# Expert blocks in order of token count, three of them with high and low halves side by side as one stationary operand

## The chip, the core and the metric

The kernel runs on one NeuronCore of a Trainium2 chip. The time is the device time of one execution in microseconds (us), median of several runs.

## What is computed

A decoder trunk of two layers for 256 tokens of 1024 channels: a mixer (convolution, pooling, mLSTM), cross-attention into 256 memory tokens, and a channel mixer that is a dense SwiGLU in the first layer and a mixture of experts in the second. The change touches the experts alone. Cut to them:

```python
logits = xt @ router_w                      # xt: 256 tokens x 1024
top_v, top_e = lax.top_k(logits, 2)         # two of eight experts a token
gate = jax.nn.softmax(top_v, axis=-1)
# rows are packed into blocks of 128 that each belong to one expert
def expert_block(args):
    xblk, e = args
    return (jax.nn.silu(xblk @ w1[e]) * (xblk @ w3[e])) @ w2[e]
y = segment_sum(yb * slot_w[:, None], slot_tok, num_segments=256)
```

w1 and w3 are 1024 x 3584 for each expert, w2 is 3584 x 1024, all float32. With the inputs that the reference makes, the reference's router gives the eight experts 76, 57, 68, 47, 42, 82, 54 and 86 rows.

## The kernel before, in words

**Precision.** A product of float32 matrices is made of three fp32r matmuls: each operand is split into a high half (a copy rounded to fp32r, by ScalarE) and a low half (the difference, by VectorE), and high x high, high x low (activation low with weight high) and low x high (activation high with weight low) are added up in PSUM. The helper `three` does this, lines 1898 to 1900.

**The expert stage** begins about 1010 us into the span and takes the rest. There are eight blocks, one for each expert in the order of their numbers; each holds up to 128 rows (`SLOTS`). Should an expert have more, further blocks follow after the eighth; there are none with these inputs.

A block is 42 chunks of weights (`ESEQ`, `N_EXP`), each 128 x 2048 floats, 1 MB. They come in seven groups: two chunks of w1, two of w3, and, from the second group on, two of w2 that belong to the group before; the last w2 chunks come at the end. A chunk goes through four hands, each an engine with its own queue in program order:
- SP issues the load (`expert_load`, line 596) into one of six buffers (`e_raw`: three named raw, then mem_t, area and xf), as soon as the buffer's last chunk has been split by VectorE.
- ScalarE makes the high half (`e_split`, line 771) into one of three `w_hi` buffers, as soon as TensorE is done with the chunk three back.
- VectorE makes the low half (`lo`, line 1214) into one of three `w_lo`.
- TensorE multiplies (`e_chunk`): 4 k-tiles or column parts by three matmuls of 512 columns, 12 a chunk. The activations (`x_hi`, `x_lo`, or `hid_e`) are the stationary operand, 128 x 128, the weights the moving one.

In ScalarE's and VectorE's queues the splits are mixed with what must be done with results (`e_post`). In step t they split chunk t and do the post work of chunk t-3; as a rule the split stands first. Post work of a group: SiLU of the w1 result out of PSUM (line 1134), the product with the w3 result (line 1747), then a **turn**: TensorE transposes the 128 x 512 product (`turn`, line 2317, four transposes, issued behind the second w1 chunk of the next group), ScalarE takes the high half (line 1139) and VectorE the low half, which the w2 chunks need.

At the end of a block ScalarE scales half of the output rows by the gates (line 1121), VectorE the other half (line 1735), and POOL adds the 128 rows to a sum in DRAM by an indirect DMA (line 714). The next block's rows are selected ahead of time (`select`, `slot_rows`), fetched by another indirect DMA on POOL (line 710), turned by TensorE (`turn_rows`, line 2399) and split (`gather_hi`, line 1115; `gather_lo`). Before the last block VectorE makes the tables for further blocks (`further_blocks`, lines 1823 to 1839). Blocks 0 to 6 are a loop on each engine; the last, with the final norm behind it, is written out.

## Time and profile before

| | |
|---|---|
| Time, median of 3 runs | 1989.75 us (1989.38 to 1990.35) |
| Span of the profiled execution | 1986.5 us |
| Instructions in it | 31923 |
| TensorE busy | 1969.3 us, 99% |
| VectorE busy | 1638.9 us, 82% |
| ScalarE busy | 1288.2 us, 65% |
| DMA, mean over the span | 268 GB/s |
| Granted TensorE clock, mean | 0.999 |
| Splits of weights by VectorE, mean | 2260 to 2292 ns |

The time of a run includes the launch and the end around the program; the profiled execution has no time of its own in the results, so its span of 1986.5 us stands beside the runs' median of 1989.75 us. In the page PE is TensorE's matmuls, PEld its weight loads, DVE VectorE, ACT ScalarE, POOL GpSimd, SP the engine that issues loads. Matmuls overlap in the records, so a matmul's record is longer than the distance to the next one's start. Tiles bear the names under which they were allotted: a_hi and a_lo hold the activations' halves, z_sig the hidden product, h the rows, k_t and u_pad small tables.

### The profile page before, as it was taken

Reading aid. Unit: us, or ns where it says so; the run is one execution under the profiler, and the core shown is the slowest. Engines: PE = TensorE matmul, PEld = TensorE weight load, DVE = VectorE, ACT = ScalarE, POOL = GpSimd, SP = SyncE. Lnnn points to the kernel's source line nnn. Section 1 sums busy time; section 2 is a strip of 40 time slices with the busy share of each in tenths; the row PEclk is TensorE's granted clock in tenths of the full one; section 3 lists DMA queues with packets and bytes.
Section 4 is the critical chain, followed back from the end, with each engine's and each line's share of the span. In section 5 each row is a group of like instructions: output and inputs, shape, how many; then the busy total and the mean of one; then the engine's idle time right before and its main releaser. Section 6 shows DMA issues by size and latency. Waiting matters only on the chain.

```text
span 1986.5 us, 31923 instructions
## 1 busy us (share of the span) xinstructions
PE 1969.3 (99%) x12185; PEld 1767.6 (89%) x12185; DVE 1638.9 (82%) x1702; ACT 1288.2 (65%) x1155; POOL 46.3 (2%) x89
## 2 busy tenths in 40 slices
PE   9999999999999999999999999999999999999998
PEld 8999999989999999999988888888888888888886
DVE  6999967577778988976578888988989888888986
ACT  7666555444436666564467777878778787777775
POOL 0000000000000000000000000000000000000000
PEclk9999999999999999999999999999999999999999
DMA  8545556445555545555479999999999999999994
GB/s 269 171 133 184 166 173 199 143 160 194 192 176 170 170 133 170 191 182 186 136 290 382 374 381 384 361 385 358 388 379 369 381 362 385 372 380 385 359 392 170
DMA packets 311377, 533.26 MB, mean 268 GB/s; under 512 B 14363, under 2 KB 157363, under 8 KB 311271
## 3 DMA queue, kind: packets, MB, share of 16 engines
q1 hardware_dynamic: 308550, 523.71, 74.8%
q0 software_dynamic: 2720, 8.08, 1.5%
q8 instruction: 73, 1.20, 0.3%
q14 instruction: 34, 0.27, 0.0%
HBM read 526.30 MB, written 7.34 MB: 269 GB/s over the span
## 4 chain that ended last, share of the span: by engine, by line
PE 88%; DVE 6%; ACT 2%; issue 2%; SPq 1%; DMA 0%; DVEq 0%; ACTq 0%
PE ps L1898 26%; PE ps L1900 26%; PE ps L1899 26%; PE ps L2213 4%; DVE w_lo L1214 2%; PE ps L2215 2%; ACT w_hi L764 1%; PE ps L2317 1%; DVE c L1281 1%; PE ps L2067 1%; PE ps L2087 1%; DVE xf L1299 0%; PE ps L2399 0%; PE ps L2033 0%; SPq L511 0%
## 5 line engine op out<-in xcount | busy, mean ns | idle before, releaser
L1214 DVE TENSOR_TENSOR w_lo<-raw,w_hi 128x2048 fp32r<-128x2048 f32 (+1 forms) x330 | 745.2, 2260 | 190.4 <-ACT w_hi L764 131.1
L1898 PE MATMUL ps<-w_hi,a_hi 128*128 128x512 f32 (+1 forms) x1472 | 568.0, 386 | 1.1 <-DVE w_lo L1214 1.1
L1900 PE MATMUL ps<-w_hi,a_lo 128*128 128x512 f32 (+1 forms) x1472 | 560.8, 381 | 0.0
L1899 PE MATMUL ps<-w_lo,a_hi 128*128 128x512 f32 (+1 forms) x1472 | 559.8, 380 | 0.0
L1898 PE MATMUL ps<-a_hi,w_hi 128*128 128x256 f32 x1456 | 416.2, 286 | 2.0 <-DVE a_lo L1569 1.6
L1899 PE MATMUL ps<-a_lo,w_hi 128*128 128x256 f32 x1456 | 411.9, 283 | 0.0
L1900 PE MATMUL ps<-a_hi,w_lo 128*128 128x256 f32 x1456 | 411.8, 283 | 0.0
L771 ACT ACTIVATE w_hi<-raw 128x2048 fp32r<-128x2048 f32 x168 | 322.3, 1919 | 119.8 <-PE ps L1900 119.2
L764 ACT ACTIVATE w_hi<-raw 128x2048 fp32r<-128x2048 f32 x157 | 296.3, 1894 | 56.7 <-PE ps L1900 52.1
L1898 PEld LDWEIGHTS ps<-w_hi,a_hi 128*128 128x128 f32 x1472 | 276.7, 188 | 54.5 <-DVE w_lo L1214 3.7
L1900 PEld LDWEIGHTS ps<-w_hi,a_lo 128*128 128x128 f32 x1472 | 276.5, 188 | 53.8
L1899 PEld LDWEIGHTS ps<-w_lo,a_hi 128*128 128x128 f32 x1472 | 276.9, 188 | 50.7 <-issue 0.2
L1898 PEld LDWEIGHTS ps<-a_hi,w_hi 128*128 128x128 f32 x1456 | 278.9, 192 | 3.7 <-issue 2.0
L1899 PEld LDWEIGHTS ps<-a_lo,w_hi 128*128 128x128 f32 x1456 | 279.0, 192 | 0.4
L1900 PEld LDWEIGHTS ps<-a_hi,w_lo 128*128 128x128 f32 x1456 | 278.9, 192 | 0.0
L1214 DVE TENSOR_TENSOR w_lo<-mem_t,w_hi 128x2048 fp32r<-128x2048 f32 x56 | 128.3, 2292 | 16.3 <-ACT w_hi L771 16.3
L1214 DVE TENSOR_TENSOR w_lo<-area,w_hi 128x2048 fp32r<-128x2048 f32 x56 | 128.3, 2291 | 15.6 <-ACT w_hi L771 15.0
L1214 DVE TENSOR_TENSOR w_lo<-xf,w_hi 128x2048 fp32r<-128x2048 f32 x56 | 128.0, 2286 | 15.8 <-ACT w_hi L771 15.8
L771 ACT ACTIVATE w_hi<-area 128x2048 fp32r<-128x2048 f32 x56 | 107.6, 1921 | 42.5 <-PE ps L1900 42.5
L1898 PE MATMUL ps<-b_pair,w_hi 128*128 128x256 f32 x456 | 130.3, 286 | 0.4 <-DVE b_pair L1214 0.4
L1899 PE MATMUL ps<-b_pair,w_hi 128*128 128x256 f32 x456 | 129.0, 283 | 0.0
L1900 PE MATMUL ps<-b_pair,w_lo 128*128 128x256 f32 x456 | 129.0, 283 | 0.0
(357 smaller groups left out, 2313.3 us busy)
## 6 DMA issues: line engine op xcount, KB each, us to landing
raw<-in_moe_w SPq DMA_DIRECT2D x168, 1024.0 KB, 7.0
raw<-in_w_in SPq DMA_DIRECT2D x66, 1024.0 KB, 5.2
mem_t<-in_moe_w SPq DMA_DIRECT2D x56, 1024.0 KB, 6.8
area<-in_moe_w SPq DMA_DIRECT2D x56, 1024.0 KB, 6.9
xf<-in_moe_w SPq DMA_DIRECT2D x56, 1024.0 KB, 6.7
raw<-in_ffn_w SPq DMA_DIRECT2D x33, 1024.0 KB, 5.3
raw<-in_w_mlstm_out SPq DMA_DIRECT2D x8, 1024.0 KB, 5.1
raw<-in_w_out SPq DMA_DIRECT2D x8, 1024.0 KB, 5.9
```

Of the source, the lines that this page charges most:

```text
L764: act.activation(w_hi[c % SPL][:, 0:n], raw[c % RAW][:, 0:n], ACT.Copy).then_inc(hi_done.sem, 1)
L771: act.activation(w_hi[m % SPL][:, :], e_raw[m % ERAW][:, 0:CH], ACT.Copy).then_inc(e_hi.sem, 1)
L1214: return dve.tensor_tensor(dst, whole, as_f32(hi), ALU.subtract)
L1281: ins = dve.scalar_tensor_tensor(dst, src, tap, dst, ALU.mult, ALU.add)
L1898: pe.matmul(dst, wh, xh, start=start, stop=False, skip_group_check=True)
L1899: pe.matmul(dst, wh, xl, start=False, stop=False, skip_group_check=True)
L1900: return pe.matmul(dst, wl, xh, start=False, stop=stop, skip_group_check=True)
L2067: ins = pe.matmul(ps[4 + hd % 2][:, tt * T:(tt + 1) * T], q_t[:, k, tt * P:(tt + 1) * P], k_t[:, k, :], start=(tt == 0 and e == 0), stop=( ...
L2087: ins = pe.matmul(ps[X_OUT_BANK[hd]][:, e * T:(e + 1) * T], vx[:, m, hd, e * P:(e + 1) * P], z_sig[:, 4 + 2 * (hd % 2) + m, :], start=(e = ...
L2213: pe.matmul(b[:, :].rearrange("p (a t) -> p a t", a=2), wh[:, k, cols], b_pair[:, :, k, :], start=(k == 0), stop=False, skip_group_check=True)
L2215: ins = pe.matmul(b[:, 0:T], wl[:, k, cols], b_hi[:, k, :], start=False, stop=(k == KB - 1), skip_group_check=True)
L2317: ins = pe.transpose(ps[6][:, k * P:(k + 1) * P], act_e[g % 2][:, k * P:(k + 1) * P], ident[:, :])
```

## The change

- **Order and kinds of blocks.** Block 0 stays expert 0. For the other seven, a plan on VectorE ranks experts by their count and puts the three smallest in blocks 1, 3 and 5 (`KINDS`, `PLACES`, L for light, H for heavy). SP reads the expert's number of a block from a table (`expert_of`) and so begins block 1's loads only when the plan is done. Light blocks hold 64 rows, heavy ones 128; an expert with more would get a further block (`cap` in `further_blocks`).
- **Light blocks on TensorE.** The stationary operand is 64 columns of high half beside 64 of low half (`x_both`, `hid_both`). It is multiplied by the weights' high half and by their low half: 8 matmuls of 512 columns a chunk instead of 12. The result has the high half's product in rows 0 to 63 and the low half's in rows 64 to 127.
- **Joining the two.** ScalarE copies each w1 and w3 result to SBUF (`up_copy`, `gate_copy`, 128 x 512). `turn_fold` multiplies it by a 128 x 64 matrix `fold` (two identities above each other), which turns and adds the halves: eight real fp32 matmuls of 64 columns where four transposes stood. SiLU and product then work on 128 x 256. At the block's end ScalarE copies rows 64 to 127 of the output, VectorE adds rows 0 to 63 (`y_low`), and ScalarE scales both halves of 64 rows.
- **Order in the light block's queues.** On both engines the post work of chunk t-3 stands ahead of the split of chunk t, always.
- **The loop** is over three pairs of a heavy and a light block; blocks 6 and 7, both heavy, are written out. The output addition of a light block has 64 rows.
- **Rows for the next block** are split into `x_both`, `x_hi`/`x_lo`, or what the next block's kind needs (`kinds`).
- Small: constants on POOL for the plan; one semaphore fewer for the constants, three fewer for loads.

The diff, cut to its core:

```diff
+LIGHT = 64
+KINDS = "HLHLHLHH"
+N_LIGHT = KINDS.count("L")
+N_PAIRS = 3
+N_OVER = 4
...
+def block_places():
+    light, heavy = iter(range(1, 1 + N_LIGHT)), iter(range(1 + N_LIGHT, NE))
+    return [0] + [next(light if kind == "L" else heavy) for kind in KINDS[1:]]
...
 # SP
+            sp.wait_ge(ids_done, 1)
+            with sp.Fori(1, NE - 1) as b:
+                e = expert_of(b)
+                for m in range(N_EXP):
+                    expert_load(b, m, e)
...
 # ScalarE
+            def l_post(b, j, m, kinds):
+                kind, g, i = ESEQ[m]
+                if m == N_EXP - 1:
+                    for n, done in enumerate((y_half.at(b, 1), None)):
...
+                        act.activation(y_low[:, n * 512:(n + 1) * 512], ps[4 + n][LIGHT:P, :], ACT.Copy).then_inc(l_copied.sem, 1)
+                    for n in range(2):
+                        c = slice(n * 512, (n + 1) * 512)
+                        act.wait_ge(l_y_sum.sem, l_y_sum.at(j, n + 1))
+                        act.activation(y_rows[0:LIGHT, c], y_low[:, c], ACT.Copy, scale=gate_col[0:LIGHT, :]).then_inc(ye_done.sem, 1)
+                    return
+                act.wait_ge(e_pe.sem, e_pe.at(b, m + 1))
+                if kind != "w2" and i == 1:
...
+                    act.activation(dst[g % 2], ps[(2 * g + (kind == "w3")) % 4][:, :], ACT.Copy).then_inc(l_copied.sem, 1)
...
+                if m in turned:
+                    n = turned[m]
+                    act.wait_ge(e_turned.sem, e_turned.at(b, n + 1))
+                    act.activation(act_l[n % 2], ps[6][:, 0:T], ACT.Silu).then_inc(e_silu.sem, 1)
+                    act.wait_ge(e_gated.sem, e_gated.at(b, n + 1))
+                    act.activation(hid_both[n % 2][:, :, 0, :], act_l[n % 2].rearrange("p (k s) -> p k s", k=4), ACT.Copy).then_inc(e_hid_hi.sem, 1)
...
+            def l_block(b, j, kinds):
+                for t in range(SPL, N_EXP + SPL):
+                    l_post(b, j, t - SPL, kinds)
+                    if t < N_EXP:
+                        e_split(b, t)
+                    else:
+                        e_split(b + 1, t - N_EXP)
...
 # VectorE
+                if m == N_EXP - 1:
+                    for n in range(2):
+                        c = slice(n * 512, (n + 1) * 512)
+                        dve.wait_ge(l_copied.sem, l_copied.at(j, 2 * NGE + n + 1))
+                        dve.tensor_tensor(y_low[:, c], y_low[:, c], ps[4 + n][0:LIGHT, :], ALU.add).then_inc(l_y_sum.sem, 1)
+                    return
...
+                    dve.wait_ge(e_silu.sem, e_silu.at(b, n + 1))
+                    dve.tensor_tensor(act_l[n % 2], act_l[n % 2], ps[6][:, T:2 * T], ALU.mult).then_inc(e_gated.sem, 1)
+                    dve.wait_ge(e_hid_hi.sem, e_hid_hi.at(b, n + 1))
+                    lo(hid_both[n % 2][:, :, 1, :], act_l[n % 2].rearrange("p (k s) -> p k s", k=4), hid_both[n % 2][:, :, 0, :]).then_inc(e_hid_lo.sem, 1)
...
+            def plan():
+                ch.link(dve.tensor_copy(total, ps[5][:, 32:32 + NE]))
+                ch.link(dve.scalar_tensor_tensor(key, total, float(NE), iota8, ALU.mult, ALU.add))
...
+                ch.link(dve.tensor_tensor(picked, each, which, ALU.mult))
+                ch.link(dve.tensor_reduce(by_block[:, :, 1:NE], picked[:, :, 1:NE, :], AX, ALU.add))
+                dve.tensor_copy(ids[0:1, 1:NE], ids_f[0:1, 1:NE]).then_inc(ids_done, 1)
...
+                ch.link(dve.tensor_scalar(cap, place, N_LIGHT + 0.5, -float(SLOTS - LIGHT), ALU.is_lt, ALU.mult))
...
 # TensorE
+            def turn_fold(b, j, g):
+                pe.wait_ge(l_copied.sem, l_copied.at(j, 2 * g + 2))
+                if g:
+                    pe.wait_ge(e_gated.sem, e_gated.at(b, g))
+                for n, src in enumerate((up_copy, gate_copy)):
+                    for k in range(4):
+                        c = n * T + k * LIGHT
+                        ins = pe.matmul(ps[6][:, c:c + LIGHT], src[g % 2][:, k * P:(k + 1) * P], fold[:, :],
+                                        start=(n == 0 and k == 0), stop=True, skip_group_check=True)
+                ins.then_inc(e_turned.sem, 1)
...
+                    for k in range(4):
...
+                        pe.matmul(dst, both, wh[:, c], start=(i == 0 and k == 0), stop=False, skip_group_check=True)
+                        ins = pe.matmul(dst, both, wl[:, c], start=False, stop=(i == 1 and k == 3), skip_group_check=True)
...
-            with pe.Fori(0, NE - 1) as b:
-                e_block(b)
+            with pe.Fori(0, N_PAIRS) as i:
+                e_block(2 * i)
+                l_block(2 * i + 1, i)
+            e_block(NE - 2)
             e_block(NE - 1, True)
```

How the instructions now stand, at the two places of which the prediction speaks. REGISTER_ALU rows compute a semaphore's value.

ScalarE around a turn, before: a_hi at L1139 is the high half of the turned product, z_sig at L1134 the SiLU.

```order
L771 ACTIVATE w_hi<-raw 128x2048
L1134 ACTIVATE z_sig<-ps 128x512
L1139 ACTIVATE a_hi<-ps 128x512
L768 REGISTER_ALU
L771 ACTIVATE w_hi<-mem_t 128x2048
```

and in a light block of the change (L1225 the copy of the w1 result to SBUF, L1230 the SiLU, L1232 the high half):

```order
L807 ACTIVATE w_hi<-raw 128x2048
L1220 REGISTER_ALU
L1225 ACTIVATE cacc<-ps 128x512
L1229 REGISTER_ALU
L1230 ACTIVATE z_sig<-ps 128x256
L1232 ACTIVATE a_hi<-z_sig 128x4x64
L807 ACTIVATE w_hi<-raw 128x2048
```

The SiLU moved behind the turn, next to the high half, and VectorE's product stands between the two:

```order
L1298 TENSOR_TENSOR w_lo<-raw,w_hi 128x2048
L1876 REGISTER_ALU
L1880 REGISTER_ALU
L1881 TENSOR_TENSOR z_sig<-z_sig,ps 128x256
L1298 TENSOR_TENSOR a_hi<-z_sig,a_hi 128x4x64
L1298 TENSOR_TENSOR w_lo<-raw,w_hi 128x2048
```

This is VectorE of a light block; L1881 is the product, the row behind it the low half. ScalarE's high half waits for L1881, the row behind L1881 for ScalarE's high half, and both stand ahead of the next split of their engine.

ScalarE where a light block ends (vx is `y_low`, h the rows of the output, L1155 the next block's rows):

```order
L1155 ACTIVATE a_hi<-ps 128x512
L803 ISA
L804 ISA
L807 ACTIVATE w_hi<-raw 128x2048
L1220 REGISTER_ALU
L804 REGISTER_ALU
L807 ACTIVATE w_hi<-raw 128x2048
L1214 ACTIVATE vx<-ps 64x512
L1211 REGISTER_ALU
L1214 ACTIVATE vx<-ps 64x512
L1218 ACTIVATE h<-vx,k_t 64x512 x2
L804 REGISTER_ALU
```

Before, one activation of 128 x 512 (L1121) stood there; now there are four of 64 x 512, two of which wait for VectorE, ahead of the split of the next block's chunk 2. VectorE has its two sums at the same place:

```order
L1298 TENSOR_TENSOR w_lo<-raw,w_hi 128x2048
L1873 ISA
L1874 TENSOR_TENSOR vx<-vx,ps 64x512
L1873 REGISTER_ALU
L1874 TENSOR_TENSOR vx<-vx,ps 64x512
L1308 REGISTER_ALU
L1298 TENSOR_TENSOR w_lo<-raw,w_hi 128x2048
```

They stand behind its split of chunk 1 and ahead of that of chunk 2, where one scaling of 128 x 512 stood before.

## Rows read from the trace of the kernel before

**Rows 1.** The page, parts 1 and 2: TensorE's busy time, its granted clock in 40 slices.
```profile
PE 1969.3 (99%) x12185; PEld 1767.6 (89%) x12185; DVE 1638.9 (82%) x1702; ACT 1288.2 (65%) x1155; POOL 46.3 (2%) x89
...
PEclk9999999999999999999999999999999999999999
```
**Rows 2.** Waits inside one expert block, 1133.1 to 1252.4 us: total, times, longest.
```profile
ACT w_hi L771 <- PE ps L1900: 25.7, 36, 1.3
DVE w_lo L1214 <- ACT w_hi L771: 12.0, 26, 1.4
```
**Rows 3.** Windows in that block: engines' busy time, TensorE's granted clock, DMA share, GB/s.
```profile
1133.10:1252.41 119.31, 119.31 (x546) 98.48 (x545) 106.78 (x68) 91.52 (x62) 4.88 (x2) 1.00 1.02 377
1140.00:1151.50 11.50, 11.50 (x51) 9.29 (x50) 9.41 (x5) 10.46 (x7) 2.13 (x1) 1.00 1.03 339
1151.50:1164.90 13.40, 13.40 (x62) 11.05 (x61) 12.57 (x14) 9.76 (x9) 0.00 (x0) 1.00 1.05 395
1193.00:1200.00 7.00, 7.00 (x33) 5.79 (x32) 6.64 (x4) 5.40 (x3) 2.09 (x1) 1.00 0.99 359
```
**Rows 4.** Timeline of TensorE around a turn: start us, us, engine, line.
```profile
1245.41 0.39 PE L1900 MATMUL ps<-w_hi,a_lo 128*128 128x512 f32 x1
1245.64 0.60 PE L2317 MATMUL ps<-ident,z_sig 128*128 128x128 f32 x4
1246.00 0.48 PE L1898 MATMUL ps<-w_hi,a_hi 128*128 128x512 f32 x1
```
**Rows 5.** Timeline of VectorE where one block's chunks give way to the next's.
```profile
1244.56 0.68 DVE L1747 TENSOR_TENSOR z_sig<-z_sig,ps 128x512 f32<-128x512 f32 x1
1245.16 2.29 DVE L1214 TENSOR_TENSOR w_lo<-area,w_hi 128x2048 fp32r<-128x2048 f32 x1
...
1252.41 4.66 DVE L1214 TENSOR_TENSOR w_lo<-raw,w_hi 128x2048 fp32r<-128x2048 f32 x2
1256.99 0.74 DVE L1735 TENSOR_SCALAR h<-ps,k_t 128x512 f32<-128x512 f32 x1
1257.65 2.28 DVE L1214 TENSOR_TENSOR w_lo<-raw,w_hi 128x2048 fp32r<-128x2048 f32 x1
```
**Rows 6.** Timeline of ScalarE over the same stretch.
```profile
1246.34 0.60 ACT L1139 ACTIVATE a_hi<-ps 128x512 fp32r<-128x512 f32 x1 [1.21 <-PE ps L2317]
1246.83 1.91 ACT L771 ACTIVATE w_hi<-xf 128x2048 fp32r<-128x2048 f32 x1
...
1250.46 1.92 ACT L771 ACTIVATE w_hi<-raw 128x2048 fp32r<-128x2048 f32 x1
1252.83 1.92 ACT L771 ACTIVATE w_hi<-raw 128x2048 fp32r<-128x2048 f32 x1 [0.45 <-PE ps L1900]
...
1257.35 1.28 ACT L771 ACT_TABLE_LOAD   x1
```
**Rows 7.** Timeline of TensorE: the first gather, 16 fp32 matmuls in 32 passes.
```profile
1011.85 3.81 PE L2305 MATMUL ps<-vx,q_t 128*128 128x128 f32 x32 [0.55 <-ACT q_t L1170]
```
**Rows 8.** Groups by line of VectorE in that block: busy us, mean ns, idle before.
```profile
L1700 DVE TENSOR_SCALAR vx<-k_t,u_pad 128x128 f32<-128x128 f32 x2 | 0.6, 340 | 0.0
```
**Rows 9.** Timeline at the start of the first block, VectorE and TensorE.
```profile
1021.04 0.16 DVE L1850 COPY u_pad<-ps 128x8 f32<-128x8 f32 x1
1021.43 2.29 DVE L1214 TENSOR_TENSOR w_lo<-mem_t,w_hi 128x2048 fp32r<-128x2048 f32 x1 [0.23 <-ACT w_hi L771]
...
1016.42 0.50 PE L1898 MATMUL ps<-w_hi,a_hi 128*128 128x512 f32 x1
```
**Rows 10.** Timeline of VectorE ahead of the last block; waits from 1853 to 1866 us.
```profile
1856.38 0.17 DVE L1823 TENSOR_SCALAR u_pad<-u_pad 128x8 f32<-128x8 f32 x1
1856.59 0.17 DVE L1824 TENSOR_TENSOR_SCAN u_pad<-u_pad 128x8 f32<-128x8 f32 x1
...
PEld ps L1898 <- DVE w_lo L1214: 1.5, 1, 1.5
```
**Rows 11.** DMA issues from 1145.5 to 1147 us: one load, KB, us from issue to landing.
```profile
area<-in_moe_w SPq DMA_DIRECT2D x1, 1024.0 KB, 8.2
```

More of the change, by code:

```diff
@@ L314, in trunk @@
         warm = table(1)
+        key, place, cap, place_of = (table(NE) for _ in range(4))
+        plan_room = dec[:, :, :].rearrange("p a b -> p (a b)")
+        beats, chosen = (plan_room[:, f * NE * NE:(f + 1) * NE * NE].rearrange("p (a b) -> p a b", a=NE) for f in range(2))
+        picked = plan_room[:, 2 * NE * NE:(2 + 1 + 3 * TT) * NE * NE].rearrange("p (r a b) -> p r a b", r=1 + 3 * TT, a=NE)
+        fold = sb("fold", [P, LIGHT])
         ids = sb("ids", [1, 16], I32)
@@ L1156, in e_block @@
                     if first:
-                        e_post(b, t - SPL, last)
+                        e_post(b, t - SPL, last, kinds)
                     if t < N_EXP:
@@ L1752, in e_post, with e_block, next_rows @@
                     lo(hid_e[n % 2][1].rearrange("p k s -> p (k s)"), ps[6][:, :], hid_e[n % 2][0].rearrange("p k s -> p (k s)")).then_inc(e_hid_lo.sem, 1)
-                if (kind, g, i) == ("w3", 1, 1) and not last:
+                if not last:
+                    next_rows(b, m, kinds)
+            def e_block(b, last=False, kinds="L"):
+                for t in range(SPL, N_EXP + SPL):
+                    first = ESEQ[t - SPL] in POST_FIRST
+                    if first:
+                        e_post(b, t - SPL, last, kinds)
+                    if t < N_EXP:
+                        e_split(b, t)
+                    if not first:
+                        e_post(b, t - SPL, last, kinds)
+                    if t >= N_EXP and not last:
+                        e_split(b + 1, t - N_EXP)
+            def next_rows(b, m, kinds):
+                if ESEQ[m] == ("w3", 1, 1):
                     slot_gates(b)
@@ L1765, in e_block, with l_block @@
+            def l_block(b, j, kinds):
                 for t in range(SPL, N_EXP + SPL):
-                    first = ESEQ[t - SPL] in POST_FIRST
-                    if first:
-                        e_post(b, t - SPL, last)
+                    l_post(b, j, t - SPL, kinds)
                     if t < N_EXP:
                         e_split(b, t)
-                    if not first:
-                        e_post(b, t - SPL, last)
-                    if t >= N_EXP and not last:
+                    else:
@@ L1849, in _ @@
             slot_rows(0, ps[5][:, 64:67])
-            ch.link(dve.tensor_copy(total, ps[5][:, 32:32 + NE]))
+            plan()
             def tail(b):
@@ new lines, in l_block @@
+            def l_block(b, j):
+                for m, (kind, g, i) in enumerate(ESEQ):
+                    l_chunk(b, j, m)
+                    if m == ROWS_AT:
+                        slot_rows(b + 1, ps[7][:, 0:3])
+                    if kind == "w1" and i == 1 and g:
+                        turn_fold(b, j, g - 1)
+                    if (kind, g, i) == TURN_LAST:
+                        turn_fold(b, j, NGE - 1)
+                    if (kind, g, i) == ("w2", NGE - 2, 1):
+                        turn_rows(b)
```

197 lines of the change are left out of this document (139 added, 58 removed).

## Prediction

> **What bounds the kernel now.** I read the page first for the engines and the clock. TensorE is busy for 99% of the span, and its granted clock is in the top tenth in every slice [rows 1]. That alone doesn't say that it is the bound, so I took one block of the expert stage, from the start of its first weight split on VectorE to that of the next block, and asked who waits for whom. ScalarE waited 25.7 us for TensorE in it, VectorE 12.0 us for ScalarE, and TensorE next to nothing [rows 2]. TensorE has work for all 119.31 us [rows 3]. Matmuls of 512 columns start 0.23 us apart and four transposes take 0.36 us [rows 4]: 36 transposes and the slot rows come to some 4 us, and the other 115.3 us are 504 matmuls at 0.228 each. So a block is as long as TensorE needs, 119.3 us.
>
> The others are close behind, and the prediction rests on that. The DMA engines moved 377 GB/s in the block at a share of 1.02 [rows 3], which is 44.98 MB. Where nothing but weights moved and the queue was full, it was 395 GB/s at 1.05; beside the two indirect transfers 339 GB/s for 11.5 us and 359 GB/s for 7.0 us. A block that waited for DMA alone would take 18.5 us for those two stretches (6.41 MB) and 38.57 MB / 395 = 97.6 us for the rest: 116.1 us. VectorE was busy for 106.8 us of the block [rows 3].
>
> A rule speaks against the change here. The Trainium skill, "DMA: Bandwidth & Descriptors", Specifications, gives about 358 GB/s as the HBM limit of a core. By that a block could not be shorter than 44.98 MB / 358 = 125.7 us, which is above what is measured; the trace disagrees, and the measurement decides. With the page's figure a light block could gain nothing.
>
> **The light block, part by part.** A chunk goes from 12 matmuls to 8: 1.82 us instead of 2.74, 38 us of TensorE less in a block. TensorE stops being the bound, so the gain is not 38 us; the next chain sets it. I work out VectorE's, per group of six chunks, counting from the start of VectorE's split of chunk A (the second w1 chunk, behind which the turn stands). Splits follow each other at 2.20 us (a record lasts 2.29; operations of 512 columns follow at 0.60) [rows 5]. ScalarE's split takes 1.92, another operation can follow it or a copy 0.1 us before its end, and VectorE's split starts 1.95 after ScalarE's [rows 6].
> - VectorE splits A, B, C at 0, 2.20 and 4.40 and is free at 6.60.
> - TensorE has A multiplied at 2.29 + 0.06 + 7 x 0.228 + 0.39 = 4.3. Then the fold: eight real fp32 matmuls, which go in two passes each. 32 such passes took 3.81 us [rows 7], so 16 take 1.8: done at 6.1. ScalarE's SiLU of 256 columns (0.37 by the slope between 512 and 2048 columns) is done at 6.5.
> - VectorE's product 6.60 to 7.0, ScalarE's high half 7.05 to 7.45, and only behind it ScalarE's split of D, at 7.37. VectorE's split of D starts at 9.32, not 6.60.
> - E, F and the next A: 11.5, 13.7 and 15.9.
>
> A turn so costs VectorE 2.7 us, most of it waiting, because product, high half and the next split stand in one line over two in-order engines; before, turns lay under TensorE's time. A group takes 15.9 us against 17.0, seven groups 111.
>
> At the start, the heavy block's last matmul slot ends at T0 = 1255.2; VectorE's splits of chunks 1 and 2 then start at T0 - 0.4 and T0 + 2.45 [rows 5]. The split of chunk 41 starts at 2.45 + 39 x 2.20 + 7 x 2.7 + 1.55 = T0 + 108.8. The 1.55 is row selection and slot rows: two operations of 0.34 [rows 8] and six of 0.1 to 0.2. They were free under TensorE and now count.
>
> **The handover to the heavy block** loses part of it. Behind split 41 VectorE first takes two x parts (1.2 us); chunk 0 reaches TensorE 5.75 us after the start of split 41, at T0 + 114.55, 1.6 us after TensorE ran dry. Then the output: where one ScalarE and one VectorE operation stood there are now two ScalarE copies, two VectorE sums behind split 1, and two scalings, all ahead of ScalarE's split of chunk 2. They have 64 rows by 512 columns; I price them as the 512-column operations of 128 rows, the nearest rows (0.5 on ScalarE, 0.6 on VectorE). Counted from split 41: sums at 7.8 and 8.4, scalings at 8.5 and 9.1, split 9.65, VectorE's split 11.6 to 13.9. TensorE has used up chunks 0 and 1 at 11.2: 2.75 us idle. The table load of 1.28 us at the loop's head [rows 6] costs another 0.35 in that thinner lead. The heavy block takes 119.3 + 3.1. A pair takes 114.55 + 122.4 = 237.0 instead of 238.6: **1.6 us less, three times: -5.0**.
>
> DMA: VectorE's chain goes round in 114.8 us, the floor is 116.1. I charge the difference, 1.3 us a light block: **+3.9**. Its bounds: 0, if the lead hides it (before, landed chunks waited at least about 4.5 us for their split: a chunk's ring time is 6 x 2.84 less 4.3 us of splitting, 12.7, of which a long landing took 8.2 [rows 11]); and 3.6, if a group's burst counts in full too (five splits at 2.20 against a chunk in 2.66: 2.3 us). I take the lower middle since the light ring time, 11.6, leaves only 3.4 of lead.
>
> **Once each.** The plan adds eleven VectorE operations ahead of split 3. Chained small ones cost 0.20 [rows 10]; the two over about 400 elements 0.6 each; in sum 2.5 us. Split 3 starts at 1023.75 instead of 1021.43 and ends at 1026.0, where TensorE, from 1016.42 on [rows 9], wants it at 1024.7: **+1.4** (bounds 0 and 2.5). The tables for further blocks grow by three chained operations and by a fourth of three kinds, 1.0 us, where TensorE already waits 1.5 [rows 10]: **+1.0**. POOL's memsets and the fold matrix come long before, SP's register loads of the expert's number come while two or three transfers are under way: nothing, or, with that cover gone, about the 0.4 of an issue. TensorE's wait on the constants now covers POOL's nine more small operations, hidden likewise. The bytes are the same but for half the rows of three output additions.
>
> **Sum:** -5.0 + 3.9 + 1.4 + 1.0 = +1.3. The span is 1986.5; the median of the runs is 1989.75, 3.2 above it. So 1991.0 us: no change, since about 0.2% (4 us) is what a measurement of this kernel can tell.
>
> **Rivals.**
> - *DMA becomes the bound (slower).* It decides from where a chunk lands later than 11.6 us after its issue. For it: the share of 1.02 now, and no block in which the queue regains lead. Against: each heavy block behind a light one is 6 us longer than DMA's floor. At 3.6 a light block instead of 1.3: +6.9, 1998.
> - *The turn's wait isn't there (faster).* If SiLU, product and high half fall into waiting that is there anyway, VectorE's chain falls to some 101 us and DMA alone limits, less the 3 us of lead that it can use up: 113 a round instead of 116.1. -5.0 - 3 x 1.8 + 2.4 = -8, 1982. For it: VectorE had 12 us of waiting in a block. Against: the order of the two queues, which the part on the change shows.
> - *The clock falls in light blocks (slower).* TensorE would have some 80 us of work in 115, in pieces of 1.8 us; no stretch of the trace shows it that idle at work. At 1.2 GHz a chunk takes 8 x 0.456 = 3.6 us, a light block 36 us more: about 2100. The Trainium skill, "TensorE: Matmul & The Clock Gate", HAM oscillation, describes this for a kernel that waits for DMA between short bursts; no run here shows it yet. The waits here are about 1 us, mostly shorter than a burst, so 4%.
> - *The change doesn't do what it says:* a light place given to an expert with over 64 rows would add a block of some 119 us. The three smallest counts are 42, 47 and 54, so no.
>
> **Numbers.** Forecast 45%, DMA bound 27%, no turn wait 21%, clock 4%, other 3%. A turn that is dearer by 0.3 (hops between engines that I put at 0.05) would add 6 us to either slow case, 2004; the fast case reaches 1981. Of the forecast's own spread (1986 to 1996) a part lies beyond either bound. Faster 0.22, same 0.41, slower 0.37.
>
> **What would show it.** Right: light blocks of 114 to 117 us from first split to first split, group after group of 16, in which VectorE waits for ScalarE behind each turn; two stalls of TensorE, 1.6 and 2.8 us, where a light block ends; heavy blocks of 119.3 otherwise; a clock of 1.00. Wrong: ScalarE waiting for DMA landings in light blocks; turns under 1 us or over 3.5; a clock under 1.00.

## The result, and the profile after

The changed kernel takes **2016.3 us** (median of 4 runs, 2014.1 to 2018.2) against 1989.6 for the kernel before on the same chip: a ratio of 1.0137, 95% interval 1.0123 to 1.0152. It is 26.7 us slower. The forecast was 1991.0, its range ended at 2004: both missed.

To see where the time went I cut both traces at the start of each block's first weight split on VectorE. The table has the main kernels of this study, worked out from those starts (us; L a light block, H a heavy one; the last column runs from the last block's first split to the end of the span). Each row is one execution. That of the changed kernel is the slowest of its four, so its span is 29.9 us above that of before where the medians are 26.7 apart; run 3 is shown by its fastest execution and run 11 by its slowest.

| profiled execution | block 0 | 1 L | 2 H | 3 L | 4 H | 5 L | 6 H | 7 to end |
|---|---|---|---|---|---|---|---|---|
| before (all heavy) | 139.4 | 119.3 | 119.3 | 119.3 | 119.3 | 119.3 | 119.3 | 137.5 |
| changed | 142.2 | 119.8 | 127.8 | 121.5 | 127.7 | 121.6 | 121.8 | 140.0 |
| forecast | 140.8 | 116.3 | 122.0 | 116.3 | 122.0 | 116.3 | 122.0 | 138.5 |
| written out (run 1) | 140.5 | 121.2 | 123.1 | 122.0 | 121.5 | 121.0 | 121.8 | 140.0 |
| dummy matmuls (run 3) | 142.2 | 115.6 | 126.4 | 115.6 | 126.5 | 116.0 | 121.8 | 140.1 |
| turn reordered, written out (run 7) | 140.5 | 114.0 | 125.4 | 113.4 | 125.5 | 113.4 | 124.2 | 140.1 |
| turn, output and scalings changed, written out (run 11) | 142.1 | 113.4 | 120.2 | 115.2 | 121.6 | 113.4 | 122.0 | 140.2 |

Two things stand against the forecast: light blocks are about 5 us too long, and two of the three heavy blocks behind a light one nearly 6.

The page of the changed kernel, to be read beside [rows 1]: the instructions on TensorE became fewer and it is idle for 3% more.

```profile
PE 1931.8 (96%) x11933; PEld 1720.2 (85%) x11933; DVE 1629.9 (81%) x1719; ACT 1292.4 (64%) x1198; POOL 45.0 (2%) x98
...
PEclk9999999999999999999999999999999999999999
```

The row of the clock shows nothing, since a slice is 50 us. Short windows do. These are windows of the changed kernel with the columns of [rows 3]: the first light block, the heavy block behind it, and two stretches inside.

```profile
1136.15:1255.95 119.80, 103.88 (x472) 80.54 (x471) 102.49 (x68) 93.26 (x75) 5.36 (x2) 0.96 1.02 375
1255.95:1383.74 127.79, 120.76 (x536) 98.65 (x535) 106.94 (x71) 92.12 (x65) 3.54 (x2) 0.97 0.97 345
...
1228.00:1231.40 3.40, 3.40 (x10) 2.60 (x10) 2.98 (x2) 1.97 (x2) 0.00 (x0) 0.54 1.06 400
1231.40:1236.00 4.60, 4.53 (x20) 3.43 (x19) 3.88 (x2) 3.88 (x3) 0.00 (x0) 1.00 1.02 398
```

The eighth column is TensorE's granted clock. Over the light block it is 0.96, from 1228.0 to 1231.4 it is 0.54: for nearly all of that stretch TensorE ran at 1.2 GHz, and then at 2.4 again. Over the whole execution I count 18 such stretches, 70.6 us in all; the kernel before has one, of 6.3 us, at its end. TensorE in the changed kernel, behind a light turn:

```profile
1224.46 0.39 PE L2565 MATMUL ps<-w_lo,b_pair 128*128 128x512 f32 x1
1226.70 0.49 PE L2551 MATMUL ps<-w_hi,a_hi 128*128 128x512 f32 x1 [1.86 <-DVE w_lo L1298]
...
1227.73 0.63 PE L2551 MATMUL ps<-w_hi,a_hi 128*128 128x512 f32 x1
1228.16 0.63 PE L2552 MATMUL ps<-w_lo,a_hi 128*128 128x512 f32 x1
1228.58 0.63 PE L2551 MATMUL ps<-w_hi,a_hi 128*128 128x512 f32 x1
```

TensorE stood idle for 1.86 us, waiting for VectorE's split; one us into the next chunk its matmuls start 0.43 us apart instead of 0.23. What opened that wait is the turn. VectorE and then ScalarE of the changed kernel at another turn of the same block:

```profile
1171.97 0.41 DVE L1881 TENSOR_TENSOR z_sig<-z_sig,ps 128x256 f32<-128x256 f32 x1
1172.87 0.42 DVE L1298 TENSOR_TENSOR a_hi<-z_sig,a_hi 128x256 fp32r<-128x256 f32 x1 [0.48 <-ACT a_hi L1232]
1174.68 2.29 DVE L1298 TENSOR_TENSOR w_lo<-raw,w_hi 128x2048 fp32r<-128x2048 f32 x1 [1.38 <-ACT w_hi L807]
```

```profile
1171.52 0.38 ACT L1230 ACTIVATE z_sig<-ps 128x256 f32<-128x256 f32 x1 [1.14 <-PE ps L2534]
1172.42 0.42 ACT L1232 ACTIVATE a_hi<-z_sig 128x256 fp32r<-128x256 f32 x1 [0.51 <-DVE z_sig L1881]
1172.74 1.90 ACT L807 ACTIVATE w_hi<-raw 128x2048 fp32r<-128x2048 f32 x1
```

This is the line that the forecast drew: SiLU, product, high half, and only then ScalarE's split. From product to split VectorE takes 2.71 us, forecast 2.7. Waits in the same light block of the changed kernel (total, times, longest), beside [rows 2]:

```profile
PE ps L2551 <- DVE w_lo L1298: 12.9, 7, 2.3
DVE w_lo L1298 <- ACT w_hi L807: 11.0, 12, 1.4
ACT z_sig L1230 <- PE ps L2534: 10.7, 7, 3.8
```

TensorE waits for VectorE there, as forecast. The third row is the loss coming back: where the clock fell, the chunk and the fold take longer, and ScalarE waits for the fold, up to 3.8 us. No wait of ScalarE for a weight load is among the block's waits.

The handover from the light to the heavy block, ScalarE of the changed kernel, beside [rows 6]:

```profile
1253.37 3.71 ACT L807 ACTIVATE w_hi<-raw 128x2048 fp32r<-128x2048 f32 x2
1257.11 1.08 ACT L1214 ACTIVATE vx<-ps 64x512 f32<-64x512 f32 x2
1261.06 1.34 ACT L1218 ACTIVATE h<-vx,k_t 64x512 f32<-64x512 f32 x2 [2.88 <-DVE vx L1874]
1262.31 1.90 ACT L807 ACTIVATE w_hi<-raw 128x2048 fp32r<-128x2048 f32 x1
1267.21 1.28 ACT L807 ACT_TABLE_LOAD   x1 [3.00 <-issue]
1268.50 1.92 ACT L807 ACTIVATE w_hi<-mem_t 128x2048 fp32r<-128x2048 f32 x1
```

ScalarE waits 2.88 us for the two sums, splits chunk 2, and then does nothing for 3.00 us, with no engine to blame, before the table load at the head of the loop. In the kernel before that load followed the split directly [rows 6]. What the changed kernel does here and the kernel before doesn't is to fetch instructions. In the view of DMA transfers the window from 1125 to 1850 us has these two queues in the changed kernel, and no instruction transfer at all in the kernel before (queue, kind: packets, MB, share):

```profile
q8 instruction: 27, 0.44, 0.3%
q14 instruction: 16, 0.13, 0.1%
```

One of these 16 transfers lies in ScalarE's 3.00 us. TensorE has four waits here (0.88 and 1.66 us before the two shown), that before chunk 3 being the longest:

```profile
1266.59 0.50 PE L2039 MATMUL ps<-w_hi,a_hi 128*128 128x512 f32 x1 [2.17 <-DVE w_lo L1298]
...
1272.80 0.80 PE L2039 MATMUL ps<-w_hi,a_hi 128*128 128x512 f32 x1 [3.20 <-DVE w_lo L1298]
```

### The profile page after: what moved, and what is told of

The parts are those of the page before. It is cut to its first block, busy times and chain, and to the rows that moved or that the text cites. A ratio compares the mean times of both kernels' runs of the same rounds, so it can differ in the third digit from the quotient of the medians.

```text
span 2016.4 us, 31516 instructions
## 1 busy us (share of the span) xinstructions
PE 1931.8 (96%) x11933; PEld 1720.2 (85%) x11933; DVE 1629.9 (81%) x1719; ACT 1292.4 (64%) x1198; POOL 45.0 (2%) x98
## 4 chain that ended last, share of the span: by engine, by line
PE 72%; DVE 14%; ACT 7%; issue 5%; SPq 1%; DMA 0%; DVEq 0%; ACTq 0%; POOL 0%
PE ps L2039 18%; PE ps L2041 18%; PE ps L2040 18%; DVE w_lo L1298 9%; ACT w_hi L807 4%; PE ps L2354 4%; PE ps L2356 2%; PE ps L2551 2%; DVE c L1365 1%; PE ps L2552 1%; ACT w_hi L800 1%; PE ps L2534 1%; PE ps L2564 1%; PE ps L2565 1%; PE ps L2458 1%
## 5 line engine op out<-in xcount | busy, mean ns | idle before, releaser
L2039 PE MATMUL ps<-w_hi,a_hi 128*128 128x512 f32 (+1 forms) x968 | 372.6, 385 | 21.4 <-DVE w_lo L1298 21.4
L2041 PE MATMUL ps<-w_hi,a_lo 128*128 128x512 f32 (+1 forms) x968 | 366.7, 379 | 0.0
L2040 PE MATMUL ps<-w_lo,a_hi 128*128 128x512 f32 (+1 forms) x968 | 366.3, 378 | 0.0
L2039 PEld LDWEIGHTS ps<-w_hi,a_hi 128*128 128x128 f32 x968 | 183.8, 190 | 58.1 <-DVE w_lo L1298 21.7
L2041 PEld LDWEIGHTS ps<-w_hi,a_lo 128*128 128x128 f32 x968 | 183.7, 190 | 34.5
L2040 PEld LDWEIGHTS ps<-w_lo,a_hi 128*128 128x128 f32 x968 | 183.9, 190 | 32.2 <-issue 0.2
L2564 PE MATMUL ps<-w_hi,b_pair 128*128 128x512 f32 x336 | 136.9, 407 | 7.5 <-DVE w_lo L1298 6.2
L807 ACT ACTIVATE w_hi<-xf 128x2048 fp32r<-128x2048 f32 x56 | 107.3, 1916 | 42.7 <-PE ps L2041 21.2
L2565 PE MATMUL ps<-w_lo,b_pair 128*128 128x512 f32 x336 | 131.8, 392 | 0.0
L2039 PE MATMUL ps<-b_pair,w_hi 128*128 128x256 f32 x456 | 130.3, 286 | 0.4 <-DVE b_pair L1298 0.4
```

Source lines behind the costliest of these rows:

```text
L807: act.activation(w_hi[m % SPL][:, :], e_raw[m % ERAW][:, 0:CH], ACT.Copy).then_inc(e_hi.sem, 1)
L2039: pe.matmul(dst, wh, xh, start=start, stop=False, skip_group_check=True)
L2040: pe.matmul(dst, wh, xl, start=False, stop=False, skip_group_check=True)
L2041: return pe.matmul(dst, wl, xh, start=False, stop=stop, skip_group_check=True)
L2564: pe.matmul(dst, both, wh[:, c], start=(i == 0 and k == 0), stop=False, skip_group_check=True)
L2565: ins = pe.matmul(dst, both, wl[:, c], start=False, stop=(i == 1 and k == 3), skip_group_check=True)
```

## The experiments

Two suspects: the clock, and the loop's head. The first four runs take one each, and two controls. The kernel before had 1989.0 us beside the first four, 1989.3 beside the next, 1989.4 beside the last.

**1. The pairs of blocks written out.**

```diff
-            with act.Fori(0, N_PAIRS) as i:
+            for i in range(N_PAIRS):
```
(and so on VectorE, TensorE and POOL)

> The three pairs of blocks are written out on ScalarE, VectorE, TensorE and POOL in place of the loop; nothing else changes. In the changed kernel a heavy block behind a loop's end took 127.8 and 127.7 us from first to first VectorE split, the one behind the loop 121.8. Theory A (the way back to the loop's head costs time now that ScalarE has no lead there, 3.0 us of 'issue' ahead of its table load): blocks 2 and 4 fall to about 122, so some 12 us less, 2004. Theory B (the difference comes from the lost clock, or from the plan of the blocks): they stay within 1 us of 127.7, 2016.

Measured: 2004.3 us (2002.3 to 2006.6), ratio to before 1.0074 (1.0057 to 1.0090), 12.0 less than the changed kernel. Heavy blocks 123.1, 121.5 and 121.8. In the profiled executions block 0 gives 1.7 us of it, where the clock fell once in the changed kernel and not here. ScalarE at the handover of this kernel:

```profile
1260.38 1.34 ACT L1218 ACTIVATE h<-vx,k_t 64x512 f32<-64x512 f32 x2 [2.87 <-DVE vx L1874]
1261.62 1.90 ACT L807 ACTIVATE w_hi<-raw 128x2048 fp32r<-128x2048 f32 x1
1263.43 1.89 ACT L807 ACTIVATE w_hi<-mem_t 128x2048 fp32r<-128x2048 f32 x1
```

The split of chunk 3 follows that of chunk 2 after 1.81 us, where it took 6.19. The wait for the sums is as it was. So the head of the loop costs ScalarE 4.4 us a pass, and two heavy blocks stand behind one; the third, behind the loop's end, had 121.8 in the changed kernel already. Besides the pause, both table loads of a pass are gone (that at the head and one ahead of the first SiLU, 1.28 us each). The heavy block of 123.1 is the one in which the clock fell, for 3.4 us; in the other two it didn't.

**2. No light blocks.** The change's order, plan and tables, every block heavy.

```diff
-KINDS = "HLHLHLHH"
+KINDS = "HHHHHHHH"
```

> Experts still in order of count, with the plan and the expert numbers read by SP, but all eight blocks heavy, in a loop of seven as before. Theory A (the loss lies in the light blocks and the handover behind them): 2.4 us for plan and tables over the kernel before, 1992; every block 119.3 us, clock 1.00. Theory B (reading the expert's number, or the order, costs in every block): blocks over 120, 1995 or more.

Measured: 1993.2 us (1991.2 to 1994.2), ratio 1.0021 (1.0011 to 1.0031). Six blocks of 119.3, at a clock of 1.00. A pass of its loop is one block again, as before the change; its table load stands at each head, with 0.02 us of idle time ahead of it, and from 1200 to 1850 us there is no instruction transfer. Ordering, plan and tables cost 4 us, the other 23 are in the light blocks and behind them.

**3. TensorE kept at work at the turns.**

```diff
                     l_chunk(b, j, m)
+                    if kind == "w3" and i == 1 and g:
...
+                        for _ in range(14):
+                            pe.matmul(ps[7][:, T:2 * T], x_both..., b_lo..., start=True, stop=True)
```

> In a light block TensorE gets 14 matmuls of 256 columns behind the second w3 chunk of groups 1 to 6, whose result nobody reads; they fall into its wait of 2.25 us behind a turn and take about 1.75. They compute nothing of the output. Theory A (each such wait brings the granted clock down to 1.2 GHz for a while, and that costs the turns and chunks after it): the granted clock in light blocks goes from 0.94 to 0.96 up to 0.99 or more, and the light blocks from 121.5 to about 117, so 2016 to some 2004. Theory B (the light block is VectorE's chain, and the clock costs nothing on it): the clock rises and the light blocks stay at 121 us; 2016.

Measured: 2001.6 us (1999.9 to 2003.7), ratio 1.0067 (1.0050 to 1.0083), 14.7 less than the changed kernel, for work that nobody reads (and one wait more, for the bank that it writes). Windows of this kernel: the turn shown above, the first light block and the heavy block behind it.

```profile
1226.00:1231.40 5.40, 5.21 (x22) 3.66 (x21) 5.40 (x3) 4.55 (x3) 0.00 (x0) 1.00 1.05 395
...
1136.23:1251.81 115.58, 110.16 (x556) 87.49 (x555) 102.37 (x68) 93.55 (x75) 5.36 (x2) 1.00 1.04 385
...
1251.81:1378.23 126.42, 119.25 (x536) 97.62 (x535) 106.87 (x70) 92.16 (x65) 3.55 (x2) 0.99 0.98 357
```

The granted clock is 1.00 through the light block, and the block has 115.58 us, between the chain of VectorE that the forecast worked out (114.8 a round) and the forecast with its DMA term (116.3). With the clock whole the excess of the light blocks is gone. The heavy block keeps 126.4, and in it the clock still fell, for 3.4 us against 6.8 in the changed kernel. Its first chunk shows that TensorE too pauses behind the loop's head, without an engine to wait for:

```profile
1255.37 0.49 PE L2039 MATMUL ps<-w_hi,a_hi 128*128 128x512 f32 x1 [2.49 <-issue]
```

**4. The light output behind the next block's split of chunk 2**, loop kept.

```diff
                 for t in range(SPL, N_EXP + SPL):
-                    l_post(b, j, t - SPL, kinds)
+                    if t < N_EXP + SPL - 1:
+                        l_post(b, j, t - SPL, kinds)
...
+                l_post(b, j, N_EXP - 1, kinds)
```

> At the end of a light block ScalarE and VectorE split chunk 2 of the next block before they copy, add and scale the output, not after. Theory A (TensorE's second stall in a handover is this chain): the stall of 2.1 us ahead of chunk 2 goes, chunk 2's split on VectorE comes some 3.5 us earlier, and each of the three heavy blocks behind a light one gets 2 to 3 us shorter: 2016 to 2009. Theory B (the stall only moves on to the loop's head and the table load behind it): under 2 us in all.

Measured: 2017.9 us (2017.4 to 2020.0), ratio 1.0144 (1.0127 to 1.0161): nothing gained. ScalarE of this kernel, ahead of the split of chunk 3:

```profile
1265.11 1.34 ACT L1218 ACTIVATE h<-vx,k_t 64x512 f32<-64x512 f32 x2 [3.21 <-DVE vx L1876]
1271.12 1.28 ACT L807 ACT_TABLE_LOAD   x1 [4.67 <-issue]
```

The idle time in front of the table load grew from 3.00 to 4.67 us. So ScalarE comes to the head later and then stands longer. TensorE waits 7.5 and 8.2 us there, and the two heavy blocks behind a head have 128.7 and 129.5 us.

**5. Written out, with the dummy matmuls.** (Edits 1 and 3.)

> The three pairs written out, and fourteen dummy matmuls of 256 columns (their result is read by nobody) at each light turn, so that TensorE does not idle there. Theory A (the clock and the loop's head are two separate losses): the gains of the two single edits, 12 us and 14.7 us, add up: about 1990 us, light blocks 115.5, heavy blocks 121 to 122. Theory B (both spend the same lead, so that either edit alone recovers most of what there is): about 1998 us.

Measured: 1993.3 us (1991.5 to 1996.3), ratio 1.0019 (1.0009 to 1.0028). That is 23.0 less than the changed kernel, where 26.7 was the sum of the single gains and 18 what theory B gave: mostly two separate losses. Light blocks 116.9, 115.7 and 115.8, heavy ones 121.5, 123.1 and 123.4; the clock fell once, for 3.4 us, in each of the last two and not in the first.

**6. Written out, output later.** (Edits 1 and 4.)

> The three pairs written out, and a light block's output (two copies, two sums, two scalings) moved behind the split of chunk 2 of the next block. Theory A (without the loop's head ScalarE reaches that split in time, so the stall at the handover goes): heavy blocks behind light ones 119.5 to 120.5 in place of 121.5 to 123, in sum 4 to 7 us less than written out alone, about 1999 us. Theory B (the output is as late for TensorE, whose first w2 chunk or whose banks wait for it, or the stall only moves to the next split): 2004 us, as written out alone.

Measured: 2004.6 us (2003.6 to 2004.9), against 2004.3 for written out alone. Theory B. Heavy blocks 122.6, 121.0 and 121.3 are 0.5 less each, inside the scatter, and TensorE still stands for 2.0 us before chunk 3.

**7. Written out, splits ahead of the turn's halves.** In a light block ScalarE and VectorE, having made SiLU and product, split the next chunk first and then make the high and the low half.

```diff
                     l_post(b, j, t - SPL, kinds)
                     if t < N_EXP:
                         e_split(b, t)
+                        l_post(b, j, t - SPL, kinds, True)
```
(with `True` the high or the low half of the turn, and without it all else)

> The three pairs written out, and in the light block ScalarE's and VectorE's split of the next chunk moved between the turn's product and its high and low half. Theory A (the turn's line over two in-order engines is what opens TensorE's gap, and the gap is what lowers the clock): VectorE's split of the chunk behind a turn starts 0.9 us sooner, TensorE's gap falls from 2.3 to about 1.4 us and its granted clock stays whole there; light blocks 115 to 117 us in place of 121, in sum about 15 us less than written out alone, 1989 us. Theory B (the clock falls at a gap of 1.4 us as well, and the chain is only 0.9 us shorter a turn, 6 us a block, part of it taken by the DMA bound): light blocks 118 to 119, about 1997 us. Theory C (the low half, now later, holds up TensorE's w2 chunks): no gain, 2004 us.

Measured: 1992.9 us (1989.6 to 1997.3), ratio 1.0017 (1.0007 to 1.0027), 11.4 less than written out alone. Light blocks 114.0, 113.4 and 113.4, less than any theory gave. TensorE behind two turns of this kernel, the third and the last of a block, and then the window and two waits of its first light block:

```profile
1191.08 0.47 PE L2561 MATMUL ps<-w_hi,a_hi 128*128 128x512 f32 x1 [1.48 <-DVE a_hi L1303]
...
1248.35 0.47 PE L2561 MATMUL ps<-w_hi,a_hi 128*128 128x512 f32 x1 [2.31 <-DVE a_hi L1303]
```

```profile
1135.30:1249.32 114.02, 98.77 (x463) 75.18 (x462) 102.65 (x68) 92.44 (x74) 4.92 (x2) 1.00 1.03 385
```

```profile
ACT w_hi L807 <- DMA raw<-in_moe_w: 8.3, 10, 1.1
...
ACT w_hi L807 <- DMA xf<-in_moe_w: 4.2, 5, 0.9
```

Behind a block's first six turns the longest wait is 1.5 us; behind its last it is 2.3, and yet the clock is 1.00 in the block. ScalarE now waits for weight loads, 10 to 14 us a light block, as it does, with 6 to 15 us, in runs 8, 10, 11 and 12: the DMA bound shows. The heavy blocks are longer than in run 1, 125.4, 125.5 and 124.2. That isn't DMA: no wait for a load is among theirs. TensorE waits 3.1 us ahead of chunk 2 in each, and the clock fell for 17 us in the three together against 3.4 in run 1. By half of the difference, an estimate, that is 6.8 of the 8.7 us that they are longer.

**8. All of it, with ten dummy matmuls.** (Edits 1, 3, 4, 7.)

> All together: pairs written out, turns reordered, ten dummy matmuls at each light turn, light output behind the split of chunk 2. Theory A (the losses found are all there is besides the start and the tables): light blocks at the DMA bound or just under it, 114 to 116, heavy 119.5 to 120, about 1981 us, under the kernel before. Theory B (a light block cannot go below what DMA and the two indirect transfers allow, and what it gains is given back in the heavy block): pairs of 238 to 239, about 1992 us.

Measured: 1987.1 us (1984.4 to 1992.3), ratio 0.9990 (0.9981 to 1.0000), between the two theories. Light blocks 113.5, 114.5 and 113.4, heavy ones 123.7, 123.7 and 123.5. ScalarE of this kernel at the handover:

```profile
1253.80 1.08 ACT L1221 ACTIVATE vx<-ps 64x512 f32<-64x512 f32 x2
1257.19 1.34 ACT L1225 ACTIVATE h<-vx,k_t 64x512 f32<-64x512 f32 x2 [2.31 <-DVE vx L1888]
1258.43 1.90 ACT L807 ACTIVATE w_hi<-mem_t 128x2048 fp32r<-128x2048 f32 x1
```

The split of chunk 3 waits behind two scalings, and these behind sums that VectorE makes after its splits. That is the next thing to take away.

**9. The loop's head moved behind a heavy block.**

```diff
+            e_block(0)
             with act.Fori(0, N_PAIRS) as i:
-                e_block(2 * i)
                 l_block(2 * i + 1, i, "H")
-            e_block(NE - 2, False, "H")
+                e_block(2 * i + 2, False, "LH")
```
(and so on VectorE and TensorE)

> The loop is kept, but its head is moved: the first heavy block stands ahead of it, and a pass is now a light block and then a heavy one, so that the head lies behind a heavy block on ScalarE, VectorE and TensorE (a heavy block prepares its rows in both layouts, two ScalarE and two VectorE operations more). Theory A (the head costs its 3 us only where ScalarE has no lead, which is behind a light block): about as much as writing the pairs out, 2004 us plus 1 for the two layouts, block 0 at 140.5. Theory B (each pass of a loop costs the same wherever its head lies): 2016 us, as the changed kernel.

Measured: 2009.1 us (2006.2 to 2010.7), ratio 1.0099 (1.0082 to 1.0115): 7.2 less than the changed kernel, 4.7 more than written out. Nearer to A. Heavy blocks have 122.2, 123.9 and 122.3, light ones 122.6, 120.5 and 121.0. ScalarE of this kernel where the second pass begins, between the splits of chunks 2 and 3:

```profile
1382.35 1.91 ACT L807 ACTIVATE w_hi<-raw 128x2048 fp32r<-128x2048 f32 x1
1385.93 1.92 ACT L807 ACTIVATE w_hi<-mem_t 128x2048 fp32r<-128x2048 f32 x1 [1.67 <-PE ps L2565]
```

There is no table load, and the 1.67 us ahead of chunk 3 are put down to TensorE, which by the waits of this stretch has an idle time without a cause itself:

```profile
PE ps L2564 <- issue: 1.3, 1, 1.3
```

So the head is not free here either, but cheaper. Two things changed at once: the place of the head, and the table loads, of which this loop has none and that of the changed kernel two a pass. The run does not part them.

**10. Head moved, turns reordered, output later, scalings on VectorE.** (Edits 9, 7, 4 and this one; ScalarE also waits for the scalings before it copies the next block's gates.)

```diff
-                        act.activation(y_rows[0:LIGHT, c], y_low[:, c], ACT.Copy, scale=gate_col[0:LIGHT, :]).then_inc(ye_done.sem, 1)
+                        dve.tensor_scalar(y_rows[0:LIGHT, c], y_low[:, c], gate_col[0:LIGHT, :], None, ALU.mult).then_inc(ye_done.sem, 1)
```

> The moved loop head, turns reordered, a light block's output behind the split of chunk 2, and its two scalings given from ScalarE to VectorE, so that ScalarE waits for nobody there. No dummy matmuls. Theory A (the 2.3 us in which ScalarE waits for VectorE's sums ahead of chunk 3 are what opens TensorE's gap of 2.9 us at the handover): light blocks 113.5, heavy ones 121.5 to 122.5 in place of 123.7, about 1984 us. Theory B (the lead of the splits over TensorE is spent at the end of a light block whatever the order, so the gap stays): 1989 us or more.

Measured: 1981.9 us (1979.1 to 1984.8), ratio 0.9959 (0.9945 to 0.9973). Theory A: light blocks 114.3, 114.8 and 113.5, heavy ones 121.9, 122.3 and 120.8, and TensorE's wait ahead of chunk 3 is 0.4 us where run 8 had 2.6. Against run 8 the head moved and the dummy matmuls went as well, so no run prices the scalings alone; run 11 against run 8, 6.8 us less, has both the scalings and the missing dummy matmuls in it.

**11. The same, written out instead of the head moved.**

> The same with the pairs written out instead of the loop's head moved. Theory A (head behind a heavy block costs nothing): within 1.5 us of the version with the moved head, which has two operations of each engine more in a heavy block. Theory B (the moved head still costs part of its 3 us a pass): 4 us or more faster than it.

Measured: **1980.3 us** (1979.5 to 1983.2), ratio 0.9955 (0.9938 to 0.9972), 1.6 from the tenth run, where theory A had 1.5 at most and theory B 4 or more: A, by and large. This is the fastest kernel of the study, 9 us under the kernel before. A window for its first light block, one for the heavy block behind it, and ScalarE at the handover:

```profile
1135.65:1249.03 113.38, 98.59 (x463) 75.10 (x462) 102.45 (x69) 92.00 (x74) 5.10 (x2) 1.00 1.04 384
...
1249.03:1369.18 120.15, 119.49 (x544) 98.16 (x543) 107.43 (x73) 89.14 (x61) 9.20 (x2) 1.00 1.02 379
```

```profile
1254.06 1.08 ACT L1222 ACTIVATE vx<-ps 64x512 f32<-64x512 f32 x2
1255.04 1.91 ACT L807 ACTIVATE w_hi<-mem_t 128x2048 fp32r<-128x2048 f32 x1
```

Nothing stands between the copies and the split of chunk 3 any more. That first pair takes 233.5 us, the other two 236.7 and 235.3, against 238.6 before.

**12. Head moved and turns reordered alone.** (Edits 9 and 7.)

> Loop head moved and turns reordered, output as in the changed kernel. Against the version with everything it prices the output's order and the scalings' engine. Theory A (output order matters now that nothing else stands in ScalarE's way): 1992 to 1994 us, 5 or more above the version with everything, heavy blocks 125. Theory B (it does not): within 2 us of it.

Measured: 1993.2 us (1990.3 to 1996.4), ratio 1.0020 (1.0010 to 1.0030). Theory A: 11.3 above the tenth run, heavy blocks 124.8, 126.1 and 124.8. The output's place, worth nothing in the fourth and the sixth run, is together with the scalings' engine worth 11 us here.

## Why the prediction was wrong

The profiled execution is 29.9 us above that of before, where the sum had +1.3. The excess of 28.6 is 14 in the light blocks, 11.3 in the heavy ones behind them, and 3 at the two ends; 0.3 lies ahead of block 0.

- **The chain of the turn (a group of 15.9 us): right.** Turns took 2.71 us on VectorE from product to split, forecast 2.7. With the clock whole the light blocks had 115.6 to 116.0 us, forecast 115.0 without the DMA term. That VectorE would set the pace and that the turn's wait would be there was shown by the seventh run, which takes part of it away and gains 11.4 us.
- **"The waits here are about 1 us, mostly shorter than a burst, so 4%": the step that failed.** It was wrong twice. The waits of TensorE are not spread but gather at the turn, 1.9 us and more at six of a block's seven; that follows from the forecast's own numbers, in which VectorE's split of D starts 2.7 us late, but I spread the idle time evenly over the chunks. And the rival was priced all or nothing, a whole block at 1.2 GHz and 2100 us, so that a small chance kept it out of the sum. The trace shows stretches instead: 3 in the first light block and 5 in each of the others. Changed, less dummy matmuls, is 4.2, 5.9 and 5.6 us for the three blocks. The other kernels with the same turns say so too: over the 15 light blocks of the changed kernel and of runs 1, 4, 6 and 9, those with 3 such stretches have 119.4 to 120.5 us, those with 4 121.0 to 121.2, with 5 121.4 to 121.6, with 6 122.0 to 122.6. Ahead of such a stretch the row showed TensorE idle for 1.86 us between bursts. The Trainium skill, "TensorE: Matmul & The Clock Gate", HAM oscillation, describes the pattern: bursts of matmuls with a wait behind each, after which the next burst starts at the low clock. By that section the trace agrees in kind; there the wait is for DMA, here it was for VectorE, the clock fell 0.3 to 1.1 us into the burst and not at its start, and 13 of 21 light turns had it, not each.
- **"The table load of 1.28 us at the loop's head costs another 0.35": the second step that failed.** I read [rows 6], in which the load followed a split without a pause, as the head's price. It was the price of another loop. A pass of the loop before was one block; a pass of the changed one is two. The first moved no instructions from its second pass on (1125 to 1850 us), nor did that of run 2; the second did in every pass. In the changed kernel and in runs 3 and 4 ScalarE comes to a head behind a light block six times. It stands idle for 3.0 to 5.1 us each time, in each of these pauses lies one instruction transfer of 8 KB on queue 14, and the table load starts 1.4 to 1.6 us behind its landing; at the twelve heads of the kernel before and of run 2 there is 0.02 us of idle time and no transfer. So no lead hid the head's price before: there was none. Written out, the kernel moves nearly as many (141 transfers in the span against 149) and has no such pause, so fetching costs where the loop jumps back. No run varied the length of a pass alone, so this is read from the traces and not tested.

  In time: two heavy blocks have 127.8 instead of 122.0, the third, which has no head, 121.8. Written out, all three have 121.5 to 123.1. Part of it is clock here too: it fell for 6.8 us in each of the two blocks, which by half, an estimate, is 3.4 of their 6 us. In run 9 the head stands elsewhere, the two loads of a pass are gone, and 7.2 of the 12 us come back, though two operations of each engine were added.
- **The two stalls, 1.6 and 2.75 us: the size right as a sum, not as a picture.** Without the head (run 1), the heavy blocks are 122.2 on average, forecast 122.4 less the part of it that lies ahead of the cut, 122.0. But TensorE waits 1.0, 1.3 and 2.6 us there, three times and not twice, and in the changed kernel four times.
- **DMA, +3.9: wrong for this kernel.** No light block waited for a load; the other losses covered it. It shows in kernels whose light blocks are shorter: those of run 7, at 113.4 to 114.0, wait for loads, and have the 113 of the rival "the turn's wait isn't there", DMA's floor less the lead used up. That the heavy block must give this back isn't so: in run 11 the light blocks have 113.4 to 115.2, and the heavy ones behind them 120.2 to 122.0.
- **Plan, +1.4, and tables, +1.0.** Block 0 had 140.5 us (run 2 140.8) in the runs with the clock whole at 1012 us, 1.1 above before: right. In the changed kernel itself, and in four others, the clock fell there too (0.50 from 1012.7 to 1016.1), another 1.7 us. The last block is 2.5 longer, 1.0 forecast; behind the wait for the tables TensorE ran at 0.50 from 1889.9 to 1893.3. The second run has both ends and 4 us, where 2.4 were forecast.
- **Sums of the forecast that don't come out.** Eleven operations of the plan at the prices given are 3.0 us, not 2.5; in run 1 the plan put the split off by 2.3. TensorE's "80 us of work in 115" leaves out the forecast's own seven folds of 1.8; with them it is 89.

So the gain that the change is made for is there: 9 us in run 11. It takes another order of a turn's halves, of the output and of the splits, another engine for two operations, and no loop's head behind a light block. Run 10 keeps a loop and has 7.5 us of it.

Left open: why ScalarE's pause at the head grew from 3.0 to 4.7 and 5.1 us in run 4, and why the clock fell behind 13 of the light turns and not behind the others, whose waits look alike. In the first light block it fell behind a wait of 1.86 us and not behind one of 2.34, so the length of the wait alone doesn't decide it.

## What to carry to other kernels

When an edit takes work from the bounding engine, draw its idle time where it will stand, not as an average: gaps that gather behind one dependency can lower TensorE's clock and so cost more than their length, and cheap dummy work shows within one run if they do. A cost that reads as zero in the profile holds for the form in which it was read: the head of a loop over one block cost nothing here, that of a loop over two cost a fetch of instructions in each pass, and the list of DMA transfers tells them apart. Price it anew when the edit changes that form, and an output step too when the edit uses up the lead that hid it. In a line over two in-order engines, put the long step that others wait for ahead of the short ones that nobody needs yet.

## What the runs showed that was not expected

- TensorE's granted clock fell to 0.5, which is 1.2 GHz, behind waits of 1.9 us between bursts of matmuls, and came back while TensorE worked on; in run 7, with 1.5 us at most at the same places, it stayed at 1.00, though a wait of 2.3 us closed each light block.
- A loop's head cost ScalarE 4.4 us a pass, and nothing to be seen in the kernel before. The loop over two blocks fetched instructions in every pass, 43 transfers from 1125 to 1850 us, and the loop over one block none.
- Weights came at 384 to 385 GB/s over whole light blocks of 113 to 116 us, against 377 in a block before [rows 3].
